# Seven weight remainders per feed-forward group computed by GpSimd instead of VectorE

## The reference

```python
hf = _rmsnorm(h, norm_ffn_g[l]) @ w_ff1[l]
h = h + jnp.square(jax.nn.relu(hf)) @ w_ff2[l]          # first block
...
y = jnp.square(jax.nn.relu(m @ w_up[l])) @ w_down[l]    # second block
x = x + rmsnorm(y, norm_post_mlp[l])
```

## Time and profile before

| what | value |
|---|---|
| median of 3 runs | 1613.94 us (1613.41 to 1614.24) |
| profiled execution | 1614.24 us, span 1612.4 us |
| mean granted TensorE clock | 0.991 |
| busy TensorE, VectorE, ScalarE, GpSimd | 95%, 75%, 44%, 35% |
| feed-forward groups with Strassen | 2 x 6, the first from about 640 to 893 us, the second from about 1239 to 1508 us |

### The profile page before, as it was taken

The page is one execution under the profiler, slowest core; times in us unless marked ns, Lnnn a source line. Parts: engine busy times, 40 slices in busy tenths (PEclk is TensorE's granted clock), DMA queues, the critical chain, the costliest instruction groups (busy, mean ns, idle before and its releaser), DMA issues. The chain is left out here.

```text
span 1612.4 us, 20830 instructions
## 1 busy us (share of the span) xinstructions
PE 1537.0 (95%) x7290; PEld 1261.1 (78%) x7290; DVE 1204.0 (75%) x1946; ACT 706.0 (44%) x1174; POOL 569.4 (35%) x251
## 2 busy tenths in 40 slices
PE   8999999999999999899999989999999889999997
PEld 6888888777888878777777868777779667877787
DVE  5689999877775457998888774867646888888735
ACT  5553333434553455443444244455745444443231
POOL 3454444322244423333332234523534223222432
PEclk9999999999999999999999999999999999999999
DMA  5333333221423313233332223211122323332122
GB/s 206 98 117 97 99 92 96 73 66 54 130 92 95 101 53 131 90 93 105 98 90 74 73 72 99 78 60 60 40 66 105 105 79 105 105 102 82 40 91 79
DMA packets 41427, 144.74 MB, mean 90 GB/s; under 512 B 4596, under 2 KB 6772, under 8 KB 41080
## 3 DMA queue, kind: packets, MB, share of 16 engines
q1 hardware_dynamic: 40320, 139.94, 27.8%
q10 hardware_dynamic: 1016, 3.62, 0.6%
HBM read 141.43 MB, written 2.11 MB: 89 GB/s over the span
## 5 line engine op out<-in xcount | busy, mean ns | idle before, releaser
L524 POOL TENSOR_TENSOR w_lo<-w_raw,w_hi 128x1024 fp32r<-128x1024 f32 x202 | 518.4, 2574 | 964.8 <-ACT w_hi L1408 964.5
L636 PE MATMUL bank<-a_hi,w_hi 128*128 128x512 f32 (+1 forms) x1120 | 445.7, 398 | 4.5 <-DVE a_lo L2948 2.3
L636 PE MATMUL bank<-a_hi,w_lo 128*128 128x512 f32 (+1 forms) x1120 | 431.7, 385 | 0.0
L636 PE MATMUL bank<-a_lo,w_hi 128*128 128x512 f32 (+1 forms) x1120 | 431.2, 385 | 0.0
L1408 ACT CAST w_hi<-w_raw 128x1024 fp32r<-128x1024 f32 x207 | 214.0, 1050 | 212.5 <-DMA w_raw<-in_stream 212.3
L636 PEld LDWEIGHTS bank<-a_hi,w_hi 128*128 128x128 f32 x1120 | 210.6, 188 | 51.9 <-issue 3.6
L636 PEld LDWEIGHTS bank<-a_lo,w_hi 128*128 128x128 f32 x1120 | 210.6, 188 | 45.4 <-issue 3.6
L636 PEld LDWEIGHTS bank<-a_hi,w_lo 128*128 128x128 f32 x1120 | 210.3, 188 | 42.5
L636 PE MATMUL bank<-dn_rest,f_hi 128*128 128x512 f32 x336 | 132.6, 395 | 0.0
L1678 ACT CAST dn_first<-dn_raw 128x1024 fp32r<-128x1024 f32 x48 | 49.2, 1049 | 148.7 <-DVE dn_raw L2413 148.2
L636 PE MATMUL bank<-b_hi,w_hi 128*128 128x512 f32 (+1 forms) x256 | 96.4, 376 | 5.3 <-DVE b_lo L2573 5.3
(11 more groups left out here) (405 smaller groups left out, 2768.8 us busy)
## 6 DMA issues: line engine op xcount, KB each, us to landing
w_raw<-in_stream SPq DMA_DIRECT2D x207, 512.0 KB, 3.6
dn_raw<-in_stream SPq DMA_DIRECT2D x48, 512.0 KB, 3.6
res<-in_xT ACTq DMA_DIRECT2D x1, 2048.0 KB, 8.2
out_y<-y_out SPq DMA_DIRECT2D x16, 128.0 KB, 1.7
x_raw<-in_xT SPq DMA_DIRECT2D x3, 512.0 KB, 8.5
mem_raw<-in_memT SPq DMA_DIRECT2D x1, 1024.0 KB, 12.0
mrow<-m_rows ACTq DMA_DIRECT2D x4, 256.0 KB, 3.1
w_raw<-in_stream SPq DMA_DIRECT2D x2, 256.0 KB, 4.1
```

The lines of the kernel that those rows point to most:

```text
L524: nc.gpsimd.tensor_tensor(w_lo[:, j, :], w_raw[:, j, :], w_hi[:, j, :].bitcast(F32), ALU.subtract).then_inc(w_lo_done, 1)
L636: return nc.tensor.matmul(o, l, r, start=start, stop=stop)
```

## The change

GpSimd gets a function `rest` that makes the seven `dn_rest` of a group in the order L11, S1, S3, S2, L22, L12, S4, and VectorE's `weight_rest` goes. In the steady groups GpSimd runs `rest(s, g)` ahead of the remainders of the next four chunks. In the second feed-forward the first remainder, L11 of group 0, stands between the remainders of chunks FF2+4 and FF2+5, the other six between FF2+5 and FF2+6. S1 and L11 wait for the third sum (S2), L22 for the second, S2 and L12 for the fourth (S4). VectorE's S4 moves from the head of `ff_half` behind the first even block; in groups 0 and 1 of the second feed-forward S2 moves behind the first odd block. ScalarE casts chunk FF2+5 behind the first even casts.

```diff
@@ gpsimd
+            def rest(s, g, names=BY_ORDER):
+                q = HALVES * s + g
+                for name in names:
+                    n = SLOT[name]
+                    pool.wait_ge(sems["apart_hi"], APART + PRODUCTS * q + n + 1)
+                    if name in ("L11", "S1"):
+                        pool.wait_ge(sems["dn_sum"], 4 * q + 3)
+                    elif name == "L22":
+                        pool.wait_ge(sems["dn_sum"], 4 * q + 2)
+                    elif name in ("S2", "L12"):
+                        pool.wait_ge(sems["dn_sum"], 4 * q + 4)
+                    nc.gpsimd.tensor_tensor(dn_rest[:, n, :], dn_raw[:, n, :], dn_top[n].bitcast(F32), ALU.subtract
+                                            ).then_inc(sems["apart_lo"], 1)
...
             for g in range(HALVES):
+                rest(0, g)
                 for c in range(CH["FF1"] + 4 * (g + 1), CH["FF1"] + 4 * (g + 2)):
                     remainder(c, c % RING)
...
             remainder(CH["FF2"] + 4, 0)
+            rest(1, 0, ("L11",))
             remainder(CH["FF2"] + 5, 1)
+            rest(1, 0, BY_ORDER[1:])
             remainder(CH["FF2"] + 6, 2)
             remainder(CH["FF2"] + 7, 3)
+            rest(1, 1)
             for g in range(2, HALVES):
                 for c in range(CH["FF2"] + 4 * g, CH["FF2"] + 4 * g + 4):
                     remainder(c, c % RING)
+                rest(1, g)
@@ scalar
             top(1, 0, "L11")
-            round_to(CH["FF2"] + 2)
+            round_to(CH["FF2"] + 1)
             square_up(1, 0)
             square_up(1, 1)
             even_casts(1, 0)
+            round_to(CH["FF2"] + 2)
@@ vector: weight_rest and its seven calls in take_products and ff_half go
             def ff_half(s, g):
                 j = 4 * g
-                left_sum(s, g, "S4")
                 evict_up(s, j)
-                weight_rest(s, g, "L11")
                 even_block(s, j)
                 even_lo(s, j)
-                weight_rest(s, g, "S1")
+                left_sum(s, g, "S4")
                 evict_up(s, j + 1)
                 odd_block(s, j + 1)
-                weight_rest(s, g, "S3")
...
             even_lo(1, 2)
+            odd_block(1, 1)
             left_sum(1, 0, "S2")
-            weight_rest(1, 0, "L11")
-            weight_rest(1, 0, "S1")
-            odd_block(1, 1)
-            weight_rest(1, 0, "S3")
             odd_block(1, 3)
...
             left_sum(1, 1, "S1")
-            left_sum(1, 1, "S2")
             even_block(1, 4)
             even_lo(1, 4)
-            weight_rest(1, 1, "L11")
             evict_up(1, 6)
             even_block(1, 6)
             even_lo(1, 6)
-            weight_rest(1, 1, "S1")
             odd_block(1, 5)
-            weight_rest(1, 1, "S3")
+            left_sum(1, 1, "S2")
```

More of the change, by code:

```diff
@@ L2425, in left_sum @@
                 ins.then_inc(sems["dn_sum"], 1)
[L2427 to L2433, removed]
             def evict_up(s, j):
@@ L2498, in take_products @@
                 take(s, g, M1, a1_part, (4, 5))
-                weight_rest(s, g, "S2")
                 take(s, g, M5, a5_part, (6, 7))
-                weight_rest(s, g, "L22")
                 take(s, g, M7, y22, (0, 1))
-                weight_rest(s, g, "L12")
                 take(s, g, M6, u2_part, (2, 3))
-                weight_rest(s, g, "S4")
                 take(s, g, M4, y21, (0, 1))
```

## The result

The changed kernel takes 1676.09 us, the median of four runs (1675.38 to 1680.86), beside 1614.09 for the kernel before on the same chip: a ratio of 1.039, with a 95% interval of 1.037 to 1.041. It is slower by 62 us. The prediction said 1667 (1620 to 1690) and slower with a chance of 0.85. The profiled execution took 1679.59 us, with a span of 1677.8; its difference to the profiled execution of before is 65.4 us.

What follows compares the result with a forecast made beforehand. It took TensorE, busy 95% of the span, as the bound, so only its idle time could be won. Terms 39.6 + 8.7 + 2.1 + 3.0 = 53.4 us, added to the 1613.94 median, gave 1667 us, range 1620 to 1690.

Steps and rivals of the forecast that it cites:

- The mechanism: VectorE operations with both inputs in SBUF and GpSimd operations exclude each other for whole instructions and alternate when both queued.
- Rival A: GpSimd hardly delays VectorE's short operations, so steady groups give back 22 us: about 1583 us; chance 0.09.
- Rival B: VectorE gets two short operations through in a row, first product 1.9 us late: 1615 to 1630 us; chance 0.16.
- The steady group: Up phase held, first down product at 27.0 us instead of 21.76; group +2.8 us, plus 1.6 for clock.
- the signs named: Expected in the profile: first-product wait of about 5 us put down to `f_lo`, five VectorE lines near 2.6 us, others.
- Nine groups look like this one: Groups 1 to 5 of the first feed-forward and 2 to 5 of the second cost alike: 39.6 us together.
- For a 5.2 us stall I take 1.6: TensorE's lower clock after each steady group's late first down product costs 1.6 us, bounds 0 and 2.4.
- Group 0 of the first feed-forward: Same chain of holds: first down product at about 664.1 instead of 655.3; +8.7 us after stalls and clock.
- Groups 0 and 1 of the second: GpSimd's L11 waits for the moved sum S2, delaying chunk FF2+5 and group 1's first product: +2.1 and +3.0 us.
- Costed at nothing: Everything outside the feed-forward groups: forecast difference 0.
- Rival C: As forecast, but every stall draws a longer half clock, 2.4 us and more: 1676 to 1690 us; chance 0.12.
- the forecast's own range: Whole kernel, the forecast itself without its rivals: 1645 to 1676 us, chance 0.63.

## Why the prediction was right, and where its sizes were off

**The mechanism was right.** Whole instructions exclude each other, short ones of VectorE too, and with both queued the engines alternate: shown by the held operations, by the kernel with reads that nobody needs (+88 us) and by the one with fills (-18 us). Rival A, that short operations are hardly delayed, falls with them. Rival B, two short operations in a row, occurs where GpSimd has run out of work (851.24 and 851.59 stand behind a GpSimd remainder that ended at 850.92, at 0.43 and 0.42 us), but not while it has the next one queued: in the whole trace of the changed kernel no two `comb`, `f_lo` or sum operations of VectorE ended between two GpSimd subtractions that followed each other at once, and in 45 cases one did.

**The steady group was right.** Stepped the first product was to start at 27.0 and did at 26.97. The group was to take 43.25 + 4.4 = 47.65 us, and the seven ordinary ones took 47.7 to 48.4. The down phase lost its two stalls. Of the signs named, two came out otherwise: the wait is put down to "issue" and not to `f_lo`, and L2466 and L2448 of before were held to 1.5 and 1.2 us, not 2.6.

**"Nine groups look like this one" was wrong.** The nine groups were to lose 39.6 us and lost 51.0 (26.56 and 24.48). This step holds the larger part of the 11.4 us between. In the kernel before all nine take 43.25 us, since VectorE has 2.7 us of slack ahead of the first down product and what is particular to a group stays inside it (the reciprocal) or in the down phase. The change uses the slack up, so whatever delays the sums comes out at the end. The first down product came 3.4 us later in group 1 of the first feed-forward (the reciprocal, shown by moving it) and 4.0 us later in group 2 of the second than in the other seven: 7.2 us of the 11.4. The cause of the latter, chunk remainders that GpSimd made late and that held two sums, is read from the rows; no run moved them. That the same late remainders cost nothing in the kernel with fills shows that they are not enough by themselves.

**"For a 5.2 us stall I take 1.6" was too low.** This is the other 4.2 us of the 11.4. No product waits in the nine down phases, and at the full clock each takes 19.05 us, so what is above that is the clock's: 1.7 to 2.9 us, 2.1 on the mean, 18.6 together where 14.4 were taken. Two of them in the windows view (span, then busy and instructions of each engine, granted clock, DMA share), with waits of 5.07 and 9.09 us ahead:

```profile
906.84:927.58 20.74, 20.74 (x84) 17.02 (x85) 12.46 (x21) 5.98 (x8) 9.49 (x4) 0.92 0.00 1
1406.26:1428.23 21.97, 21.97 (x84) 17.90 (x85) 12.56 (x21) 7.02 (x9) 9.50 (x4) 0.86 0.30 90
```

**Group 0 of the first feed-forward: +8.7, measured +8.5.** The first product came at 663.40, which is 664.0 in the time of the kernel before, where 664.1 was stepped.

**Groups 0 and 1 of the second: +5.1, measured +3.8.** In time counted from the stretch's start as before, the chunk's products began at 1274.0 (forecast 1274.5) behind a wait of 9.75 us, the down phase ended at 1301.5 (1301), and group 1's first product came at 1316.7 (1316.3). The stepping was right; the sum wasn't. From 1316.3 its own steps lead to 1316.3 + 19.05 + 1.4 + 1.6 = 1338.4, which is 3.5 us behind the 1334.9 of before for both groups together. The prediction took 1.4 + 1.6 as what group 1 loses, but before, that group's down phase had stalls of its own (1.5, 2.2 and 1.5 us), and these go with the change: by the steps it loses 1.4 us net.

**Costed at nothing: +2.0 us between the feed-forwards and behind the second.** This can't be put down to the change. The stretch from the end of group 5 of the first feed-forward to the start of the second took 345.96 us before and 348.01 after, but in the ten kernels of this document it took anything from 344.09 (the one with extra reads) to 349.18 (the one with halves), and the end behind the last group 104.5 or 105.1.

**Rival C, a longer half clock at every stall,** is partly right: of the nine groups one paid 2.9 us and one 2.4, and the mean of 2.1 is above the 1.6 taken. But that is 4.2 us in nine groups, not the 9 to 18 of the rival, whose sum, 1676 to 1685, ends below the 1690 that it names. The upper end of rival B, likewise, is 1624 by its own terms and not 1630.

**The whole.** The profiled execution is 3.5 us above the median, so the sum, 12 us short of it, is 9 us short of the median. The median of 1676.09 lies just above the forecast's own range of 1645 to 1676, and the 1.6 us that the sum counted too much in the second feed-forward made up for a little of what the groups lacked.

**What the orders do.** Their 4.4 us measured alone can't be set off against the 62 of the change term by term, since in the changed kernel the same places wait for GpSimd.

## What to carry to other kernels

Work moved from VectorE to GpSimd is only off VectorE if it runs while VectorE does something that the pair of them can do together: here evictions from PSUM, not operations with two SBUF inputs. Look in the profile of before at how long the short VectorE operations take beside a GpSimd operation, place GpSimd's reading in the stretch where VectorE evicts, and cut the instructions short where they must meet. A per-group cost times the number of groups holds only while the slack in each group covers what differs between them, so look at what else runs once in each group before multiplying.

## What the runs showed of the hardware that was not expected

Equal stalls don't cost an equal clock. In the kernel with halved remainders TensorE waits 3.2 us ahead of the first down product in four groups in a row. The windows of TensorE behind two of these waits (span, then busy and matmuls of each engine, granted clock, DMA share):

```profile
853.60:857.00 3.40, 3.38 (x15) 2.81 (x16) 2.70 (x4) 0.93 (x2) 1.07 (x1) 1.00 0.03 7
760.60:764.00 3.40, 3.37 (x8) 2.72 (x9) 2.70 (x4) 0.93 (x2) 1.06 (x1) 0.50 0.00 0
```

Behind a wait of 3.21 us the granted clock is 0.50, the lower of the two levels (1.2 GHz), and eight products run in 3.4 us; behind one of 3.19 us it is 1.00 and 15 run. With waits of 3.18 to 3.21 us the four groups take 47.16, 45.85, 44.27 and 44.27 us, a spread of 2.9 us by the clock alone, from the same work. Nor is a shorter wait always free: in the kernel with the orders alone 2.44 us were followed by seven products in 2.8 us at a granted clock of 0.50, while in the kernel before 2.17 us left it full.

The exchange is lopsided. When both queues are full the engines take turns, so each pays about the length of the other's instruction: VectorE's `f_lo` takes 2.6 us for 0.42, while GpSimd's three remainders beside it take 7.47 us, where three of the 2.40 that one takes alone would be 7.2.
